# Stick-breaking attention: which operand of the weighted values stands still in TensorE

## What is computed

```python
q = rms_norm_2(qkv[:, :, 0], q_norm).transpose(0, 2, 1, 3)
k = rms_norm_2(qkv[:, :, 1], k_norm).transpose(0, 2, 1, 3)
v = qkv[:, :, 2].transpose(0, 2, 1, 3)
o = stick_breaking_attention(q, k, v).astype(x.dtype)
o = o.transpose(0, 2, 1, 3).reshape(bsz, seq, SB_HEADS * HEAD_DIM)
x = x + g_m[:, None, :] * (o @ w_out)
```

## Time and profile before

| | us |
|---|---|
| median of 3 runs | 890.99 |
| lowest and highest | 890.70, 891.02 |
| the profiled execution | 891.4 |
| its span, first to last instruction | 889.3 |
| PE busy in it | 880.2 (99%) |
| DVE busy | 694.1 (78%) |
| ACT busy | 501.6 (56%) |

### The profile page before, as it was taken

How to read it: one execution, slowest core, us unless ns; L and a number is a source line. 1 busy time by engine, 2 the same in 40 slices (tenths; PEclk the granted TensorE clock), 3 DMA queues, 4 the chain that set the end, 5 groups by cost and what they waited for, 6 DMA issues and landing times.

```text
span 889.3 us, 13261 instructions
## 1 busy us (share of the span) xinstructions
PE 880.2 (99%) x4833; PEld 747.9 (84%) x4833; DVE 694.1 (78%) x735; ACT 501.6 (56%) x673; POOL 29.0 (3%) x52
## 2 busy tenths in 40 slices
PE   8999999999999999999999999999999999999998
PEld 5998878888888799979888888878777888888886
DVE  4698977988888987896888888687797875655655
ACT  5545665565555658756554455465675565545542
POOL 4000110000000100002000000010000000000000
PEclk9999999999999999999999999999999999999999
DMA  6989585899899384565988887536434366556551
GB/s 215 338 270 341 183 302 183 319 364 369 328 332 340 129 284 145 175 202 183 364 310 316 321 313 281 195 114 211 135 118 142 118 208 195 190 189 188 189 192 67
DMA packets 117091, 208.04 MB, mean 234 GB/s; under 512 B 7236, under 2 KB 81068, under 8 KB 111928
## 3 DMA queue, kind: packets, MB, share of 16 engines
q1 hardware_dynamic: 116566, 205.31, 67.1%
q10 hardware_dynamic: 290, 2.10, 0.7%
q0 software_dynamic: 192, 0.05, 0.0%
HBM read 206.39 MB, written 1.05 MB: 233 GB/s over the span
## 4 chain that ended last, share of the span: by engine, by line
PE 93%; DVE 4%; DMA 2%; issue 1%; ACT 1%; SPq 0%; DVEq 0%; ACTq 0%
PE ub L1937 11%; PE tp L1937 10%; PE acc L1837 7%; PE acc L1838 7%; PE acc L1840 7%; PE ub L1939 5%; PE acc L1800 5%; PE tp L1939 5%; PE acc L1802 5%; PE acc L1801 5%; PE tp L1957 4%; PE acc L1957 3%; PE acc L1923 3%; PE acc L1925 3%; PE acc L1924 3%; PE ub L2183 1%
## 5 line engine op out<-in xcount | busy, mean ns | idle before, releaser
L1157 DVE TENSOR_TENSOR w_lo<-w_raw,w_hi 128x1024 fp32r<-128x1024 f32 x283 | 341.8, 1222 | 105.1 <-ACT w_hi L728 104.7
L728 ACT ACTIVATE w_hi<-w_raw 128x1024 fp32r<-128x1024 f32 x283 | 296.8, 1057 | 211.9 <-PE acc L1840 49.8
L1937 PE MATMUL tp<-aT,w_hi 128*128 128x512 f32 x432 | 135.9, 396 | 0.0
L1937 PE MATMUL ub<-aT,w_hi 128*128 128x512 f32 x432 | 135.4, 395 | 0.0
L1837 PE MATMUL acc<-w_hi,hT_hi 128*128 128x512 f32 x284 | 110.8, 390 | 0.8 <-DVE w_lo L1157 0.8
L1838 PE MATMUL acc<-w_lo,hT_hi 128*128 128x512 f32 x284 | 110.6, 389 | 0.0
L1840 PE MATMUL acc<-w_hi,hT_lo 128*128 128x512 f32 x272 | 105.8, 389 | 0.0
L1939 PEld LDWEIGHTS tp<-aT,w_lo 128*128 128x128 f32 x432 | 81.2, 188 | 19.2
L1939 PEld LDWEIGHTS ub<-aT,w_lo 128*128 128x128 f32 x432 | 81.1, 188 | 18.9
L1939 PE MATMUL tp<-aT,w_lo 128*128 128x256 f32 x432 | 84.9, 278 | 0.0
L1939 PE MATMUL ub<-aT,w_lo 128*128 128x256 f32 x432 | 84.9, 278 | 0.0
(11 more groups left out here) (324 smaller groups left out, 1307.9 us busy)
## 6 DMA issues: line engine op xcount, KB each, us to landing
ada_raw<-in_l_ada_w SPq DMA_DIRECT2D x24, 1024.0 KB, 6.7
w_raw<-in_l_ffn_w_gate SPq DMA_DIRECT2D x44, 512.0 KB, 4.7
w_raw<-in_l_ffn_w_up SPq DMA_DIRECT2D x44, 512.0 KB, 3.8
w_raw<-in_l_ffn_w_down SPq DMA_DIRECT2D x44, 512.0 KB, 3.4
w_raw<-in_w_up SPq DMA_DIRECT2D x32, 512.0 KB, 4.8
w_raw<-in_w_down SPq DMA_DIRECT2D x32, 512.0 KB, 5.4
scratch<-in_l_ada_w SPq DMA_DIRECT2D x14, 1024.0 KB, 7.4
w_raw<-in_attn_w_qkv SPq DMA_DIRECT2D x24, 512.0 KB, 6.3
```

The lines of the kernel that those rows point to most:

```text
L728: act.activation(rounded_part(v), w_raw[:, v % SLOTS, :], ACT.Copy).then_inc(hi_done, 1)
L1157: dve.tensor_tensor(rest_part(v), w_raw[:, v % SLOTS, :], rounded_part(v).bitcast(F32), ALU.subtract).then_inc(lo_done, 1)
L1937: pe.matmul(banks[f], rounded_part(v)[:, c[f]], aT[:, :, b, :], start=b == 0, stop=False)
```

## The change

`pair_weighted` swaps the operands: now the weights `stick_wT`, a full 128x128 block, stand still, and the values move, 64 columns at a time. Three matmuls for each head give an output with tokens on partitions (`stick_bank`: one bank for each tile of tokens, eight heads in a bank). Since the output projection wants features on partitions, two kinds of step come in. `Yn` copies the two banks of eight heads from PSUM to `stick_o` in SBUF, tile 0 on ACT and tile 1 on DVE. `Zn` (PE) waits for both, and transposes them in eight blocks of 128x128 back into the same banks. `On` then works as before, but waits for `so_T`, which the transpositions signal.

The list changes with it. O0 stood behind A5 and O1 behind A6; both now stand behind D6. O2 and O3 stood behind C7 and V7; both now stand behind L29. P26 is split in two: its first token tile stays `P26`, its second becomes `I26` and stands between V7 with Y1 and Z1.

```diff
...
-    P22 W4 S6 V2 V3 M6 D5 H26 C4 G6 L25 A6 O1 P23 W5 S7 E5 M7 D6 H27 C5 G7 L26 A7 D7 P24 W6 H28 L27 C6
+    P22 W4 S6 V2 V3 M6 D5 H26 C4 G6 Y0 L25 A6 P23 Z0 W5 S7 E5 M7 D6 O0 O1 H27 C5 G7 L26 A7 D7 P24 W6 H28 L27 C6
...
+                elif step == "Y":
+                    act.wait_ge(so_ready, 4 * n + 4)
+                    act.activation(stick_o[n][:, 0, :], stick_bank(n, 0), ACT.Copy).then_inc(so_copied_a, 1)
                 elif step == "O":
-                    act.wait_ge(so_ready, 2 * n + 2)
+                    act.wait_ge(so_T, n + 1)
                     bank, hi, _ = out_pairs(n)
                     act.activation(hi, bank, ACT.Copy).then_inc(so_hi, 1)
...
+                elif step == "Y":
+                    dve.wait_ge(so_ready, 4 * n + 4)
+                    dve.tensor_copy(stick_o[n][:, 1, :], stick_bank(n, 1)).then_inc(so_copied_v, 1)
                 elif step == "O":
                     dve.wait_ge(so_hi, n + 1)
                     bank, hi, lo = out_pairs(n)
...
                 for q in parts:
                     part_ready(2 * u + q, i, per)
-                    for t in range(NT):
+                    for t in tiles:
                         last = project_tile(2 * u + q, t, 2 * q, bank(t), op_hi, op_lo, h == first and q == 0,
                                             h != first and q == 1)
-                    last.then_inc(w_used, 1)
+                    if tiles[-1] == 1:
+                        last.then_inc(w_used, 1)
...
-                out = pair_out(p)
-                for v, q, w in ((0, slice(0, TOK), slice(0, TOK)), (1, slice(P, TOK), slice(TOK, SC))):
-                    for e in range(2):
-                        f = slice(SB_DH * e, SB_DH * (e + 1))
-                        last = pe.matmul(out[f, q], vtok[:, v, p * P + SB_DH * e:p * P + SB_DH * (e + 1)],
-                                         stick_wT[:, 2 * p + e, w], start=v == 0, stop=v == 1)
+                for e in range(2):
+                    c, w = slice((p % 4) * P + SB_DH * e, (p % 4) * P + SB_DH * (e + 1)), stick_wT[:, 2 * p + e, :]
+                    v = [vtok[:, b, p * P + SB_DH * e:p * P + SB_DH * (e + 1)] for b in range(2)]
+                    pe.matmul(stick_bank(p // 4, 0)[:, c], w[:, 0:P], v[0], start=True, stop=True)
+                    pe.matmul(stick_bank(p // 4, 1)[:, c], w[:, P:TOK], v[0], start=True, stop=False)
+                    last = pe.matmul(stick_bank(p // 4, 1)[:, c], w[:, TOK:SC], v[1], start=False, stop=True)
                 return last
+
+            def stick_T(n):
+
+                pe.wait_ge(so_copied_a, n + 1)
+                pe.wait_ge(so_copied_v, n + 1)
+                for m in range(2):
+                    for b in range(2):
+                        for t in range(NT):
+                            q = b * TOK + t * P
+                            last = pe.transpose(stick_bank(n, m)[:, q:q + P],
+                                                stick_o[n][:, t, (2 * m + b) * P:(2 * m + b + 1) * P], ident[:, :])
+                    last.then_inc(so_T, 1)
...
                     if n in (24, 28):
                         pe.wait_ge(so_lo, 2 if n == 24 else 4)
                     if n < 28:
-                        out_unit(U_WOUT1, OUT_LO_FIRST, n // 2 - 12, (hT_hi, hT_lo), parts=(n % 2,))
+                        out_unit(U_WOUT1, OUT_LO_FIRST, n // 2 - 12, (hT_hi, hT_lo), parts=(n % 2,),
+                                 tiles=(0,) if n == 26 else (0, 1))
                     elif n == 28:
                         out_last(U_WOUT1, OUT_LO_FIRST, sums=(8, 10))
+                elif step == "I":
+                    out_unit(U_WOUT1, OUT_LO_FIRST, n // 2 - 12, (hT_hi, hT_lo), parts=(n % 2,), tiles=(1,))
+                elif step == "Z":
+                    stick_T(n)
```

More of the change, by code:

```diff
@@ L93 @@
     P16 S0 M0 L19 G0 H20 A0 P17 T3 S1 M1 H21 D0 L20 G1 A1 P18 W0 S2 M2 D1 B3 H22 C0 G2 L21 A2
-    P19 W1 S3 M3 D2 H23 C1 G3 L22 A3 P20 W2 S4 M4 D3 H24 C2 E4 G4 L23 A4 P21 W3 S5 V0 V1 M5 D4 H25 C3 G5 L24 A5 O0
-    P22 W4 S6 V2 V3 M6 D5 H26 C4 G6 L25 A6 O1 P23 W5 S7 E5 M7 D6 H27 C5 G7 L26 A7 D7 P24 W6 H28 L27 C6
-    P25 W7 L28 V4 V5 C7 O2 H29 L29 P26 V6 V7 O3 H30 L30 P27 H31 L31 P28 K0 H32 P29 H33 P30""")
+    P19 W1 S3 M3 D2 H23 C1 G3 L22 A3 P20 W2 S4 M4 D3 H24 C2 E4 G4 L23 A4 P21 W3 S5 V0 V1 M5 D4 H25 C3 G5 L24 A5
+    P22 W4 S6 V2 V3 M6 D5 H26 C4 G6 Y0 L25 A6 P23 Z0 W5 S7 E5 M7 D6 O0 O1 H27 C5 G7 L26 A7 D7 P24 W6 H28 L27 C6
+    P25 W7 L28 V4 V5 C7 P26 H29 V6 V7 Y1 I26 Z1 L29 O2 O3 H30 L30 P27 H31 L31 P28 K0 H32 P29 H33 P30""")
 LRU_STEPS = steps("""B6 U0 H2 L2 U1 H3 E0 L3 M6 U2 H4 T0 L4 C0 B7 U3 H5 E1 L5 U4 H6 G0 L6 M7 X0 U5 H7 S0 F0 X1 G1 D0 E2
@@ L187, in block_program @@
                     ada_flat[:, UNIT + D:2 * UNIT], gate_ffn[:, :]]
+        stick_o = [scratch[:, 2048 + n * 1024:3072 + n * 1024].rearrange("p (t n) -> p t n", t=NT) for n in range(2)]
         stick_w = scratch[:, 8192:8192 + 4 * SC].rearrange("p (r n) -> p r n", r=2)
@@ L230, in chunk_banks, with stick_bank @@
             return tp[:, :, :] if c < 0 else acc[:, 2 * (c % 2):2 * (c % 2) + 2, :]
-        def pair_out(p):
-            bank = acc[:, p // 2, :] if p < 4 else ub[:, p // 2 - 2, :]
-            return bank[:, (p % 2) * TOK:(p % 2 + 1) * TOK]
+        def stick_bank(n, t):
+            return acc[:, t, :] if n == 0 else ub[:, t, :]
         def out_pairs(n):
@@ L373, in block_program @@
         so_ready = sem("so_ready")
+        so_copied_a = sem("so_copied_a")
+        so_copied_v = sem("so_copied_v")
+        so_T = sem("so_T")
         so_hi = sem("so_hi")
@@ L1803, in project_tile, with project @@
                 return last
-            def project(u, h, bank, i=None, per=0, first=0, operand=None, lo_count=0, parts=(0, 1)):
+            def project(u, h, bank, i=None, per=0, first=0, operand=None, lo_count=0, parts=(0, 1), tiles=(0, 1)):
                 op_hi, op_lo = operand or (aT_hi[:, 4 * h:4 * h + 4, :], aT_lo[:, 4 * h:4 * h + 4, :])
@@ L2017, in hidden_T, with out_unit @@
                 last.then_inc(h_T, 1)
-            def out_unit(u, order, n, operand=None, lo_count=0, parts=(0, 1)):
+            def out_unit(u, order, n, operand=None, lo_count=0, parts=(0, 1), tiles=(0, 1)):
                 c, h = order[n]
                 project(u + n, h, lambda t: acc[:, 2 * t + c, :], first=order[0][1], operand=operand,
-                        lo_count=lo_count, parts=parts)
+                        lo_count=lo_count, parts=parts, tiles=tiles)
             def out_last(u, order, lo_count=0, sums=()):
```

## The result

| | before | after |
|---|---|---|
| median of the executions, us | 890.85 (4) | 902.9 (4) |
| lowest and highest | 890.63, 891.02 | 900.32, 904.24 |
| the profiled execution | 891.4 | 900.32 |
| its span | 889.3 | 897.9 |
| outside the span | 2.1 | 2.4 |

The changed kernel takes 1.0127 times as long, with an interval of 1.0115 to 1.0139: 12 us more. The forecast was 900.1, the range 898.0 to 903.2. The profiled execution is the shortest of the four, and it matters that it is: its mean granted clock is 0.999, that of the other three 0.996 or 0.997. In its trace the low clock stands only at the span's end, where PE has nothing to do (0.50 in 896.5 to 897.9 us, 1.00 in every stretch read from 600 to 895). So this trace shows the change with TensorE's clock up; what the others add is found by the experiments.

The account below looks back on a forecast made before the run. The prediction took PE's own queue to bound the kernel. Values 4.5, transpositions 1.7 and the wait of P24 2.8 summed to 9.1 us, giving 900.1 us against 890.99, with a range of 898.0 to 903.2.

Parts of the forecast that it names:

- PE's queue is the time: Whole span: PE is busy 99%, so what is added to or taken from its queue counts in full.
- Weighted values: V0 to V7 on PE: 96 passes at 0.112 us, 10.7 us in place of 6.2, so +4.5 us.
- The rule of 29 ns: Skill's distance between warm matmuls of 64 columns, without weight load; 96 passes would be 2.8 us, this term -3.4.
- What the change gives up: Weighted values: two heads of a pair run side by side on two column halves, 1.45 us instead of 2.6.
- The change of form: First projection matmul behind scores or values is 0.43 us, not 0.23: leaving a part-array form costs 0.20.
- Transpositions: Z0 and Z1 on PE: 16 transpositions of 128x128 at 0.109 us each, +1.7 us.
- The waits of Z and of P28, and the split of P26: Copies ahead of Z0, Z1 and P28 are hidden under projection matmuls, and splitting P26 costs nothing.
- The wait of P24: PE waits behind S7 while DVE does M7, D6 and the rests of O0 and O1: +2.8 us, perhaps 2.5 to 3.2.
- The median of 900.1: Forecast for the whole changed kernel: 9.1 us added to the median before, 890.99.
- the clock's case: Rival included in the range: granted clock falls after PE's pause at P24, +2.8 us, 902.9 us; chance 6%.
- The clock falls: Rival: after the pause at P24 the clock drops to 1.2 GHz for about one projection part, +2.8, 902.9 us; 6%.
- the clock at nine tenths in every slice: Reason given against the clock's fall: in the trace before, the granted clock is nine tenths or more in every slice.

Follow-up runs that it names:

- e1: The changed kernel with O0 and O1 moved from behind D6 to ahead of M7; 898.77 us, ratio 1.0079.
- e2: The kernel before, with only O0 and O1 moved behind D6, no swapped operands and no transpositions; 895.78 us, ratio 1.0053.
- e5: The changed kernel with O0 and O1 moved further back on DVE, behind L26; 904.56 us, ratio 1.0146.
- e9: The changed kernel with O0 and O1 put between M7 and D6; 902.71 us, ratio 1.0133.
- e10: e1 with every matmul of the values split in two of 64 stationary columns, one for each half of the array; 894.74 us, ratio 1.0037.
- e4: The changed kernel with only the first 64 of 128 stationary columns in each matmul of the values; 897.95 us.
- e8: The kernel before with heads in turn, both heads of a block written into the same 64 array columns, O0 to O3 moved; 897.48 us, ratio 1.0076.
- e7: The kernel before with the two loops of the weighted values exchanged, all passes of head 0, then head 1; 891.23 us, ratio 1.0001.
- e3: The change's swapped operands without the Y and Z steps, O0 and O1 ahead of L25, output not transposed; 897.11 us, ratio 1.0063.
- e6: The kernel before with its weighted values gathered into two blocks, V0 to V3 behind S6, V4 to V7 behind P26; 890.76 us, ratio 0.9995.
- e0: The changed kernel run once more, unaltered; 902.28 us, ratio 1.0125.

## Why the prediction was right, and where it wasn't

**PE's queue is the time.** Right. The terms on PE add up to the span's growth within 0.1 us. They do so in the other traces too, if each is counted from the start of V0 to the end of the span, which leaves the scatter ahead of the change out:

| kernel | V0 to the end, us | over before | by its rows |
|---|---|---|---|
| before | 230.6 | | |
| change | 240.0 | 9.4 | 4.5 + 1.75 + 3.06 = 9.3 |
| e1 | 237.2 | 6.6 | 4.5 + 1.75 + 0.36 = 6.6 |
| e2 | 233.7 | 3.1 | 3.06 |
| e5 | 243.4 | 12.8 | 9.3 + 1.3 + 2.2 = 12.8 |
| e9 | 240.6 | 10.0 | 9.3 - 0.87 + 1.5 = 9.9 |
| e10 | 233.1 | 2.5 | 0.4 + 1.75 + 0.31 = 2.5 |

**Weighted values, +4.5.** Right: +1.22, +1.22, +1.03, +1.02, in sum 4.49, by rows of after. The price of a pass, 0.112, was taken from the first layer's values rather than from the moving columns. The reason given for it, that load and movement lie side by side and the load is the longer one, is borne out by e4, where half the columns of weights halve the pass. The Trainium skill, "TensorE: Matmul & The Clock Gate", section "LDWEIGHTS (loading the stationary operand)", gives a load as columns divided by 1.2 in ns, 107 and 53 for the two; the traces show passes of 112 and 58. The rule of 29 ns, quoted in the prediction against this change, is off by four times for these passes.

**What the change gives up.** Right, but only told apart by e8. e7 alone would have spoken against it.

**The change of form, 0.20.** Right in the sum, and a little off in its places: the matmul behind the full passes is 0.28 and not the 0.23 that the prediction named as a sign, and the blocks are 2.82 and 2.62 where it had 2.88 (with the 0.20 for leaving the scores) and 2.68. The two cancel, which is luck. Behind half the columns it is 0.43 again in e4, e8 and e10.

**Transpositions, +1.7.** 1.75. **The waits of Z and of P28, and the split of P26: nothing.** Right; no row of PE's waits in after names them.

**The wait of P24, +2.8.** The mechanism was right, the queue of four steps behind S7, and so was the range of 2.5 to 3.2. The size was 3.06, and the step that was mis-sized is the last, "some 0.04 to hand over": the chain has 0.25 us of issue between DVE's rest and PE's first matmul (in e2 and e5 too), and what the prediction had to go by was M7's 0.05 behind S7, a hand-over in the other direction. The steps before it fit: M7, D6 and the two rests come to 2.8 us.

**The median of 900.1.** This is the part that was wrong within a range that held. The sum's own terms spanned 899.4 to 900.9, and 902.9 lies 2 us above that; it is within 903.2 because the range was drawn to take in the clock's case. The profiled execution gave 900.32 and the other one with its clock up 901.83. But that is not the likeliest case, it is two of eight. The rival "The clock falls", put at 6% with 902.9 us, is what happened in most executions, and it came out at 902.9 and 902.28. The step that failed is the reason against it: the clock at nine tenths in every slice says nothing about a pause that the trace of before doesn't contain. The prediction said that no such pause lay behind the start, and should have drawn from it that the row had no vote. Its price, +2.8 for a whole part at half speed, was somewhat high: 1.4 us in P24 in e4's trace, 1.5 in e9's, 2.2 in e5's, since the low stretch covers only a part of P24: in e5 and e9 it begins while PE still stands and ends within P24, in e4 it begins 1.2 us behind the pause. The six executions, 902.98 on average, lie 1.9 over the two with the clock up, 901.1, which is between these prices. So the median came to the rival's 902.9 by another sum: 1.0 us less for the fall, and 1.0 more for the longer pause, the time outside the span and scatter. That the two agree to the tenth is luck.

**Left over.** 0.3 us outside the span: 2.34 to 2.45 in all kernels that have the Y and Z steps (the change, e1, e4, e5, e9, e10), 1.99 to 2.09 in the others (e2, e3, e6, e7, e8). It goes with the Y and Z steps and not with the swap (e3 has the swap without it); by what means isn't settled. And executions of one kernel with its clock up lie 1.5 to 2.4 us apart (the change, e1), and a microsecond of that separates 901.1 from the forecast. In the traces it lies ahead of V0: 1.5 us in e0's, 2.8 in e1's, of which one wait of 1.1 us at 394 us is a part.

## What to carry to other kernels

Price a small float32 matmul by the longer of its weight load and its movement, not by its moving columns: making the large operand stand still is dear when few columns move. Before swapping operands, ask whether both halves of the array were at work; a form of 64 columns that keeps both busy beats a full one that waits for its loads. And where a change makes a saturated TensorE stand still for 2 us (0.31 to 1.10 were harmless here, 2.19 was not, and nothing between was tried), add the clock's fall to the length of the pause. Cost the order of the steps on the other engines apart from the arithmetic: here moving two rests ahead of a mask gave back 3.5 of 10.8 us.

## What was not expected of the hardware

- By the mean clock, the granted clock fell with pauses of 2.19 us (in four executions of four), 3.06 (eleven of fifteen) and 4.36 (four of four), and not once with 0.31 to 1.10 (eighteen). In the traces of e4, e9 and e5 it is at 1.2 GHz at P24, and the matmuls there took 0.43 us instead of 0.23, over 3.4, 3.2 and 4.7 us of PE's work. It fell about 2.2 us into the pause in e5, 2.0 in e9, and in e4 only when PE had been busy again for 1.2 us. That a pause cut from 3.06 to 2.19 us wins nothing was a surprise.
- PE starts passes on an idle half of its columns ahead of passes that stand before them in its queue (e7 beside e8), so the order of the two heads in the code made no difference here (891.23 against 891.26 us).
- Loads of 64 columns into the two halves run beside each other, 0.032 us a pass for 48 of them (e10). A full pass, which does twice as much, takes 0.112, so the two halves do the same work in 0.55 of the time.
- PE starts 0.25 us after DVE's last instruction where a semaphore of DVE releases it from a pause, but DVE some 0.02 to 0.05 us after PE's.
